# The last convolution tile laid out by GpSimd, and the shift's product one band sooner

## The reference

```python
def conformer_conv_module(x, norm_g, pw1_w, pw1_b, dw_w, dw_b, ln_g, ln_b, pw2_w, pw2_b):
    h = rms_norm(x, norm_g)
    u = h @ pw1_w + pw1_b
    u = u[..., :D_MODEL] * jax.nn.sigmoid(u[..., D_MODEL:])
    u = causal_depthwise_conv(u, dw_w, dw_b)          # 31 taps, one filter per channel
    u = jax.nn.silu(layer_norm(u, ln_g, ln_b))        # over the channels
    return x + u @ pw2_w + pw2_b
```

## Time and profile before

| | |
|---|---|
| three runs | 1203.08, 1203.21, 1204.93 us; median 1203.21 us |
| profiled execution | 1204.0 us, of which the span of the trace is 1202.2 us |
| TensorE busy | 1172.7 us, 98% |
| VectorE busy | 795.7 us, 66% |
| ScalarE busy | 558.6 us, 46% |
| GpSimd busy | 61.6 us, 5% |
| the chain that ended last | PE 81%, DVE 10%, ACT 6% |

### The profile page before, as it was taken

One profiled execution on the slowest core, in us unless ns is written; L12 is line 12 of the kernel. 1 busy time (PEld: TensorE's weight loads), 2 busy tenths in 40 slices (PEclk: granted clock), 3 DMA queues, 4 the chain that ended last, 5 costly groups with the idle time before them and its releaser, 6 DMA issues.

```text
span 1202.2 us, 16669 instructions
## 1 busy us (share of the span) xinstructions
PE 1172.7 (98%) x6134; PEld 994.6 (83%) x6134; DVE 795.7 (66%) x1098; ACT 558.6 (46%) x941; POOL 61.6 (5%) x77
## 2 busy tenths in 40 slices
PE   8998969999999999999999999999999999999998
PEld 7787948888888888887999999886888888888887
DVE  6999574676537663667567777876676457653763
ACT  6297864444214431344656656555444124421441
POOL 0000002000000000001212022200000000000000
PEclk9998969999999999999999999999999999999999
DMA  6897602233322333222321221221233322332222
GB/s 226 322 356 281 216 0 70 71 105 105 105 90 85 105 105 105 70 87 88 126 85 38 71 71 48 88 76 36 70 105 105 105 75 101 105 105 88 87 79 96
DMA packets 23239, 130.79 MB, mean 109 GB/s; under 512 B 2704, under 2 KB 2832, under 8 KB 12048
## 3 DMA queue, kind: packets, MB, share of 16 engines
q1 hardware_dynamic: 23184, 130.04, 31.7%
HBM read 124.74 MB, written 17.09 MB: 118 GB/s over the span
## 4 chain that ended last, share of the span: by engine, by line
PE 81%; DVE 10%; ACT 6%; issue 2%; DMA 0%; POOL 0%; SPq 0%; POOLq 0%; DVEq 0%; ACTq 0%
PE bank L1382 66%; PE bank L1544 8%; PE bank L1459 2%; DVE w_lo L894 1%; DVE conv_c L986 1%; ACT conv_c L698 1%; ACT u L682 1%; PE bank L1594 1%; PE bank L1578 1%; DVE conv_b L986 1%; DVE w_lo L902 1%; ACT w_hi L615 1%; ACT prob L856 1%; DVE small L1306 1%; PE bank L1421 1%
## 5 line engine op out<-in xcount | busy, mean ns | idle before, releaser
L1382 PE MATMUL bank<-xg_hi,w_hi 128*128 128x512 f32 x832 | 327.0, 393 | 1.8 <-DVE xg_lo L910 1.4
L1382 PE MATMUL bank<-xg_lo,w_hi 128*128 128x512 f32 x832 | 323.8, 389 | 0.0
L1382 PE MATMUL bank<-xg_hi,w_lo 128*128 128x512 f32 x832 | 323.8, 389 | 0.0
L615 ACT ACTIVATE w_hi<-w_raw 128x2048 fp32r<-128x2048 f32 x79 | 150.6, 1907 | 147.2 <-PE bank L1382 147.1
L894 DVE TENSOR_TENSOR w_lo<-w_raw,w_hi 128x2048 fp32r<-128x2048 f32 x79 | 182.7, 2313 | 32.6 <-ACT w_hi L615 32.6
L771 ACT ACTIVATE ffn_t<-ffn_u,par 128x512 f32<-128x512 f32 x88 | 71.9, 817 | 268.7 <-DVE ffn_u L1196 268.7
L1382 PEld LDWEIGHTS bank<-xg_hi,w_hi 128*128 128x128 f32 x832 | 156.2, 188 | 37.0 <-DVE xg_lo L910 1.9
L1382 PEld LDWEIGHTS bank<-xg_lo,w_hi 128*128 128x128 f32 x832 | 156.2, 188 | 33.4 <-issue 1.7
L1382 PEld LDWEIGHTS bank<-xg_hi,w_lo 128*128 128x128 f32 x832 | 156.2, 188 | 32.8
L1382 PE MATMUL bank<-act_hi,w_hi 128*128 128x512 f32 x448 | 177.1, 395 | 4.2 <-DVE act_lo L1126 4.0
L1382 PE MATMUL bank<-act_lo,w_hi 128*128 128x512 f32 x448 | 175.1, 391 | 0.0
(11 more groups left out here) (183 smaller groups left out, 1448.0 us busy)
## 6 DMA issues: line engine op xcount, KB each, us to landing
w_raw<-stream SPq DMA_DIRECT2D x87, 1024.0 KB, 4.9
band_rows<-band SPq DMA_DIRECT2D x20, 576.0 KB, 9.5
xg_band<-band_rows SPq DMA_DIRECT2D x11, 576.0 KB, 6.2
w_raw<-stream SPq DMA_DIRECT2D x8, 768.0 KB, 4.2
band_sb<-band_rows SPq DMA_DIRECT2D x6, 576.0 KB, 15.2
band<-band_sb SPq DMA_DIRECT2D x5, 624.0 KB, 10.3
x<-x_t SPq DMA_DIRECT2D x8, 256.0 KB, 6.2
out_t<-x SPq DMA_DIRECT2D x8, 256.0 KB, 2.0
```

What stands on the lines that cost most here:

```text
L615: act.activation(w_hi[:, j, :], w_raw[:, j, :], ACT.Copy).then_inc(w_hi_done, 1)
L1382: got = pe.matmul(out, weights(w, j, k, m), v[:, k, :], start=(k == first and s == 0), stop=(k == last and s == 2), skip_group_check=True)
```

## The change

GpSimd takes the 16 layout copies of tile 7. Its copies stand ahead of all its running sums, and wait for the eight gated tiles (`c_u`) and the zeros ahead of them (`pad_done`). ScalarE leaves its loop after the last sigmoid. Bands 16 to 19 wait for the new semaphore `last_split`, the others for `u_split` as before. The product that spreads the shift stands behind band 13 and no longer behind band 14.

```diff
@@ gpsimd
+            pool.wait_ge(c_u, KT)
+            pool.wait_ge(pad_done, 2)
+            for g in range(PHASES):
+                for r in range(PHASES):
+                    at = conv_u[g * CH:(g + 1) * CH, KT - 1, r:CP:PHASES]
+                    got = pool.tensor_copy(u2[r * CH:(r + 1) * CH, BANDS - PHASES + g, 0:at.shape[-1]], at)
+            got.then_inc(last_split, 1)
+
             sum_squares("ffn0")
@@ scalar
                 if 0 < m < KT - 2:
                     split_weights(m + 2, m % RING)
+                if m == KT - 1:
+                    continue
                 act.wait_ge(c_u, m + 1)
@@ tensor
-                pe.wait_ge(u_split, tile + 1)
+                if tile < len(PE_TILES) - 1:
+                    pe.wait_ge(u_split, tile + 1)
+                else:
+                    pe.wait_ge(last_split, 1)
...
-                if n == 14:
+                if n == 13:
                     pe.wait_ge(first_summed, 1)
```

More of the change, by code:

```diff
@@ L369, in trunk @@
         u_split = sem("u_split")
+        last_split = sem("last_split")
         first_summed = sem("first_summed")
```

## The result

The changed kernel takes 1196.82 us (median of five runs, 1196.65 to 1197.76), the kernel before 1203.08 us in the same session. The ratio is 0.9944, with a 95% interval of 0.9932 to 0.9955. In a later session, with five runs more, it was 1196.86 against 1203.59, ratio 0.9945 (0.9931 to 0.9958). The forecast was 1195.4, with a range to 1199.0. The profiled execution took 1196.69 us, its span is 1194.9 (before: 1204.0 and 1202.2).

What follows compares the result with a forecast made beforehand. TensorE was taken to be bound by ScalarE's late emptying of a bank before band 3, then by ScalarE's work behind band 10. 8.91 - 0.6 - 0.5 = 7.8 us off the median 1203.21 gave 1195.4, range 1193.7 to 1199.0.

Steps and rivals of the forecast that it cites:

- Part 1: Bands 3 to 5: without ScalarE's 16 copies, 6.03 us of stop and 2.88 of low clock gained, 8.91 at band 10.
- Part 2: GpSimd's 16 copies beside VectorE's taps: 0.30 us each, 4.8 in all, of which VectorE loses 1.9.
- X: Total time VectorE loses to GpSimd's 16 copies; taken as 1.9 us, with 4.8 kept as the other end.
- Part 3: Spreading product behind band 13 waits for VectorE's sum: loss X - 1.34 where positive, 0.6 us, or 3.5 for X = 4.8.
- Part 4: Start of pw2 after the statistics' stop: clock may come back later, 0.5 us lost, between 0 and 1.0.
- A: GpSimd's copies cost VectorE nothing that counts, X under 1.34, no loss at the product; 1194.3 to 1195.3 us; chance 0.25.
- B: VectorE loses 0.40 us a copy, X 6.4, TensorE stops 5.9 us at the product; 1199.9 to 1202.8 us; chance 0.06.
- C: Slower than before: 0.61 us a copy, X 9.8, loss 8.4 at the product plus clock's 2.9; 1206.1 us; chance 0.05.
- D: The stop moves: bands' matrices or two weight units load too late for the earlier bands; 1199 us; chance 0.04.

Runs made afterwards that it cites:

- the moved product: Kernel before with only the spreading product moved to behind band 13, ScalarE still laying out tile 7; 1203.86 us, ratio 1.0001.
- double copies: Changed kernel with each of GpSimd's 16 copies made a second time into a spare tile; 1201.51 us, or 1198.71 with the product behind band 14.
- memset run: Changed kernel with GpSimd's 16 copies replaced by 16 memsets of the same shapes, which write and do not read; 1195.77 us.
- product 14: Changed kernel with the spreading product back behind band 14, copies still on GpSimd; 1195.32 us, again 1195.54.
- the run with added products: Changed kernel, product behind band 14, with 29 and 17 constant products added in TensorE's two waits at the statistics; 1194.83 us.
- both edits: Changed kernel, product behind band 14, second weight unit rounded late, 25 and 16 products added in TensorE's waits at the statistics; 1193.96 us.

## Why the prediction was right, and where it was off

**Part 1, the mechanism right, the size that of one profile.** Forecast was 8.91 at band 10; from each kernel's first band it is (130.91 - 99.69) - (122.03 - 99.72) = 8.91. The loads that had to be there were there. But the 8.91 is measured against the very profile that it was read from. The same stop in the profile of the moved product had bands 3 to 5 at 7.77, and against that one the gain would be 7.8. The 6.03 of the stop are fixed, the 2.88 of low clock were one execution's.

**Part 2, the mechanism right, X too small.** Forecast X = 1.9 (0.12 a copy). From each kernel's first band it is (129.09 - 99.72) - (126.58 - 99.69) = 2.48, or 0.155 a copy; with double copies the sum's last instruction begins at 131.92 and X is (131.92 - 99.89) - 26.89 = 5.14, or 0.16 a copy. The mis-sized term is this held time, a copy's 0.30 less 0.18. The one was an estimate between two other operations, the other was read from a long addition; which of them is off stays open, as no run has these copies without VectorE's instructions beside them. The memset run shows that it is the reading. The whole record (4.8, the price that the prediction took by the rule of the Trainium skill, "SBUF — State Buffer", section "Who interferes with whom", that the pair is held for the whole instruction) was too much. The copies took 12.42 us and not 4.8, because they take turns with the taps; they ended at 115.1, and band 16 began at 134.81.

**Part 3, right with that X.** The loss was put at X - 1.34, so 1.14 for 2.48. The stage lost 1.15 against product 14. With double copies the formula gives 5.14 - 1.34 = 3.80, and with 2.37 for the clock 6.17; the stage is 6.18 longer than product 14's. With these copies and the product behind band 14 (X = 5.16) it gives 5.16 - 3.35 = 1.81; with the clock's 4.60 - 2.93 = 1.67 that is 3.48, and 3.45 was measured. That no fall of the clock was taken for the stop of 1.8 us came true, but its reason, the 1.00 at 108 to 110, was that of one execution: the moved product's profile has 0.62 there.

**Part 4, luck.** Forecast 0.5, and in the two first profiles it is 14.82 - 14.43 = 0.39. But the same stretch is 14.39 and 15.22 in two profiles of product 14, and 15.45 where only the product moved. So 0.39 is inside the scatter of single executions, and a loss by the change is not shown. What keeps it small is VectorE's pace, as the run with added products suggests; the prediction had only the clock.

**The sum.** From the bands to the statistics the gain is 57.24 - 49.56 = 7.68, which is 8.91 - 1.23. With pw2's 0.39 off that is 7.29, and the spans differ by 1202.2 - 1194.9 = 7.3; forecast was 7.8. The 0.5 is X's 0.6, less 0.1 in part 4. The medians differ by 6.3 (later 6.7), so the forecast of the time was off by 1.4 to 1.5 us. Of this second gap most is that the gain was read from an execution of 1204.0 us, 0.9 above the median of 1203.08, and subtracted from a median. In which stretch the usual execution is shorter is not shown: the kernel before has only this one profile, and the one of the moved product, with 7.77 us for bands 3 to 5, lost it again from pw2 on. That the time came out inside the range is no proof of the sizes.

**The rivals.** A (no price for VectorE) is refuted by the late sum (129.09), and by product 14 and the memset run, which win back what it costs. B and C had the right mechanism at a wrong price: with double copies the clock did fall in a stop of 4.48 us, and the time came out 4.7 us above the changed kernel's. The place of the fall and its extra cost (2.37 against the 2.9 written) were as drawn. B tied it to a stop of 5.9 us; it fell with one of 2.48 as well. D did not occur.

## What to carry to other kernels

Work moved to an idle GpSimd was not free here where it read SBUF beside VectorE instructions with two SBUF inputs: price it per instruction (here 0.16 us of VectorE's time for a copy of 32x136), and ask what waits for the end of VectorE's row. A product that waits for a late sum belongs where its wait is covered: one place too early cost 1.3 of 8.05 us here, and it looked harmless because before the change the sum had been early by 11 us. A saving that holds a stretch of low clock is to be taken from several executions, not from one.

## What the hardware showed that was not expected

- GpSimd's copies and VectorE's instructions took turns for 12.4 us, 0.78 us a copy, where 16 memsets took 4.01.
- After a stop of 1.81 us TensorE's clock stayed at 1.00; after one of 2.48 it fell to 0.50, and only when TensorE was at work again (132.38 restart; 0.80 in 132 to 134, 0.50 in 134 to 136).
- The length of the stop alone does not decide. Near the start of the program TensorE stops for VectorE in every kernel here. With added products at the statistics (first two lines) the clock fell behind a stop of 1.78 us, with both edits (last two) it stayed at 1.00 behind one of 1.99:

```profile
11.82 0.50 PE L1393 MATMUL bank<-xg_hi,w_hi 128*128 128x512 f32 x1 [1.78 <-DVE xg_lo L921]
14.00:16.00 2.00, 2.00 (x7) 1.54 (x6) 1.96 (x4) 2.00 (x4) 0.00 (x0) 0.50 1.08 437
11.77 0.50 PE L1394 MATMUL bank<-xg_hi,w_hi 128*128 128x512 f32 x1 [1.99 <-DVE xg_lo L922]
14.00:16.00 2.00, 2.00 (x11) 1.65 (x10) 1.96 (x4) 2.00 (x5) 0.00 (x0) 1.00 1.09 437
```

- This early fall goes with a beginning of the bands that is 1.1 to 1.6 us later: 101.09 and 101.14 in the two profiles that have it (0.94 over the first 30 us), 99.57 to 99.99 in the twelve others (1.00).
